# Moving one wait and one table load at the ends of a transformer kernel's feed-forward phases

## What is computed

```python
def swiglu(h, w_in, w_out):
    gate, up = jnp.split(h @ w_in, 2, axis=-1)
    return (jax.nn.silu(gate) * up) @ w_out

for l in range(DEPTH):
    h = h + 0.5 * swiglu(rms_norm_2(h, ffn1_norm[l]), ffn1_w_in[l], ffn1_w_out[l])
    h = h + hybrid_mixer(rms_norm_2(h, mix_norm[l]), ...)
    h = h + 0.5 * swiglu(rms_norm_2(h, ffn2_norm[l]), ffn2_w_in[l], ffn2_w_out[l])
return rms_norm_2(h, final_norm)[:, META:]
```

## Time and profile before

| | |
|---|---|
| median of 3 runs | 2420.91 us (2420.75 to 2426.59) |
| profiled execution | 2424.67 us, its span 2422.7 us |
| TensorE busy, share of the span | 93% |
| TensorE's weight loads | 86% |
| VectorE, ScalarE | 68%, 49% |
| mean granted clock of TensorE | 0.961 of full speed |
| the four feed-forward phases' first products start at | 984.27, 1505.44, 1714.84, 2216.71 us |
| TensorE idle before them | 2.64, 4.06, 4.06, 4.05 us |
| TensorE idle at the two mixers' starts | 5.58 us each |
| other idle times of TensorE within the two mixers | 17, together 17.8 us |

### The profile page before, as it was taken

The page is one execution under the profiler, slowest core; times in us unless marked ns, Lnnn a source line. Parts: engine busy times, 40 slices in busy tenths (PEclk is TensorE's granted clock), DMA queues, the critical chain, the costliest instruction groups (busy, mean ns, idle before and its releaser), DMA issues. The chain is left out here.

```text
span 2422.7 us, 40671 instructions
## 1 busy us (share of the span) xinstructions
PE 2242.9 (93%) x16709; PEld 2090.7 (86%) x16709; DVE 1639.5 (68%) x2201; ACT 1186.6 (49%) x1656; POOL 100.4 (4%) x133
## 2 busy tenths in 40 slices
PE   6978899969888998899999998999999999998998
PEld 6868778859677886899888898999999888898998
DVE  5674588843847885777665656777777665656786
ACT  4744466733646774533356445333433346545333
POOL 2022000000000000000300000000000210000000
PEclk8989899989999999999999999999999999999999
DMA  8420379939125994545542234545454553344552
GB/s 219 138 87 20 108 265 338 345 102 209 36 71 203 342 335 148 175 157 174 159 142 88 89 130 163 176 162 186 138 193 156 149 154 103 105 157 160 188 189 72
DMA packets 257020, 395.53 MB, mean 163 GB/s; under 512 B 16937, under 2 KB 204194, under 8 KB 256866
## 3 DMA queue, kind: packets, MB, share of 16 engines
q1 hardware_dynamic: 251616, 380.09, 46.7%
q0 software_dynamic: 4880, 13.13, 3.1%
q10 hardware_dynamic: 370, 0.11, 0.0%
HBM read 385.43 MB, written 7.86 MB: 162 GB/s over the span
## 5 line engine op out<-in xcount | busy, mean ns | idle before, releaser
L315 PE MATMUL psum_banks<-source_high,weights_high 128*128 128x272 f32 (+1 forms) x2656 | 785.5, 296 | 56.5 <-DVE weights_low L1813 23.5
L317 PE MATMUL psum_banks<-source_high,weights_low 128*128 128x272 f32 (+1 forms) x2656 | 770.7, 290 | 0.0
L316 PE MATMUL psum_banks<-source_low,weights_high 128*128 128x272 f32 (+1 forms) x2656 | 770.6, 290 | 0.0
L315 PEld LDWEIGHTS psum_banks<-source_high,weights_high 128*128 128x128 f32 x2656 | 513.5, 193 | 66.1 <-DVE weights_low L1813 26.1
L316 PEld LDWEIGHTS psum_banks<-source_low,weights_high 128*128 128x128 f32 x2656 | 514.0, 194 | 0.8
L317 PEld LDWEIGHTS psum_banks<-source_high,weights_low 128*128 128x128 f32 x2656 | 513.3, 193 | 0.0
L1813 DVE TENSOR_TENSOR weights_low<-weight_ring,weights_high 128x2048 fp32r<-128x2048 f32 x104 | 239.3, 2303 | 186.1 <-ACT weights_high L1806 185.6
L694 DVE TENSOR_TENSOR weights_low<-weight_ring,weights_high 128x2048 fp32r<-128x2048 f32 x131 | 292.8, 2287 | 73.7 <-ACT weights_high L688 73.5
L688 ACT ACTIVATE weights_high<-weight_ring 128x2048 fp32r<-128x2048 f32 x131 | 242.4, 1912 | 191.9 <-PE psum_banks L317 181.8
L1806 ACT ACTIVATE weights_high<-weight_ring 128x2048 fp32r<-128x2048 f32 x104 | 198.5, 1909 | 43.8 <-PE psum_banks L317 34.6
L315 PE MATMUL psum_banks<-hidden_high,weights_high 128*128 128x272 f32 (+1 forms) x736 | 213.0, 289 | 0.0
(11 more groups left out here) (494 smaller groups left out, 3794.0 us busy)
## 6 DMA issues: line engine op xcount, KB each, us to landing
weight_ring<-ffn_w_in SPq DMA_DIRECT2D x88, 1024.0 KB, 6.6
weight_ring<-w_in SPq DMA_DIRECT2D x48, 1024.0 KB, 5.3
weight_ring<-ffn_w_out SPq DMA_DIRECT2D x44, 1024.0 KB, 4.9
weight_ring<-moe_w_down SPq DMA_DIRECT2D x24, 1024.0 KB, 6.9
weight_ring<-moe_w_gate SPq DMA_DIRECT2D x44, 512.0 KB, 4.8
weight_ring<-moe_w_up SPq DMA_DIRECT2D x44, 512.0 KB, 6.5
weight_ring<-gdn_w_in SPq DMA_DIRECT2D x16, 1024.0 KB, 5.8
more_ring<-moe_w_gate SPq DMA_DIRECT2D x32, 512.0 KB, 5.0
```

Source lines behind the costliest of these rows:

```text
L315: pe.matmul(out, w_hi, x_hi, start=start, stop=False)
L316: pe.matmul(out, w_hi, x_lo, start=False, stop=False)
L317: return pe.matmul(out, w_lo, x_hi, start=False, stop=stop)
```

## The change

It has two parts, both in `ffn_phase`.

TensorE's wait for the root (`relay.std`) stood ahead of the first chunk's gate products. It now stands between the two halves of the up products, ahead of the only ones that write bank 3.

ScalarE takes a root of one number per partition into a new buffer `junk` that nobody reads. It stands after the last chunk's silu and before the wait for the first finished block of `h`. The load of the root's table is put in front of it.

```diff
         squares = pr.sb(ctx, "squares", [P, KT, L])
+        junk = pr.sb(ctx, "junk", [P, 1])
...
         def gate_up_first(pe):
-            pe.wait_ge(relay.std.sem, relay.std.at(1))
             pe.wait_ge(lo_n.sem, lo_n.at(place(0, "gate") + 1))
             products(pe, 0, "gate", 0)
             products(pe, 0, "gate", 1)
             pe.wait_ge(lo_n.sem, lo_n.at(place(0, "up") + 1))
-            for m in range(2):
-                products(pe, 0, "up", m).then_inc(hm.sem, 1)
+            products(pe, 0, "up", 0).then_inc(hm.sem, 1)
+            pe.wait_ge(relay.std.sem, relay.std.at(1))
+            products(pe, 0, "up", 1).then_inc(hm.sem, 1)
...
                 for c in range(2 * pairs + 1, n_chunks):
                     step(c, c)
+                act.activation(junk[:, :], pr.eps[EPS], ACT.Sqrt)
                 for k in range(KT):
                     act.wait_ge(ad.sem, ad.at(8 * last + k + 1))
```

## The result

The changed kernel takes 2398.72 us (median of 4 runs, 2395.76 to 2399.76) against 2421.03 before (4 runs). The ratio is 0.9899, with a 95% interval of 0.9886 to 0.9913, so it is 1.0% faster: 22.3 us by the medians, 24.5 (21 to 28) by the ratio. Every ratio is to runs of the kernel before that were taken beside the runs in question. The forecast was 2397.5 in a range of 2392.5 to 2409. A second set of runs beside later experiments gave 2398.1 us and 0.9905 (0.9889 to 0.9922).

What follows compares the result with a forecast made beforehand. TensorE's own work plus its idle places were taken to bound the kernel. Wait 12.8, clock 6.7 and table loads 3.9 sum to 23.4 us: 2401.3 for the profiled execution, 2397.5 against the median, range 2392.5 to 2409.

Steps and rivals of the forecast that it cites:

- The wait: Four feed-forward starts: TensorE's 14.8 us wait for the root shrinks to 0.5 us each, gaining 12.8 us.
- the lower bound: Feed-forward starts: TensorE restarts at the earliest 0.30 us after its last sum, as ScalarE does.
- The clock: Behind the three longer gaps at feed-forward starts: the fall to half clock goes, gaining 6.7 us.
- The table loads: Loads moved ahead of the roots at two mixers' starts and the end: 1.29 us each, together 3.9 us.
- That rival (2393.6): Three table loads that count: each moved load frees as much again, 3.9 us more, because ScalarE empties first; chance 0.03.
- the one of a preload without effect: Dummy root: a load is put before each root anyway, so 19.5 us gained, 2401.4; chance 0.07.
- VectorE as the next limit: Feed-forward starts: VectorE's 5.22 us idle time is used up, leaving 0.9 us margin at TensorE's second chunk.
- rival 2: VectorE takes the wait's place: TensorE waits for weights_low or scaled halves within 15 us of phase start; 2417.0, chance 0.06.
- The panel: Feed-forward starts: a panel issued at the block's start lands in 5.1 us, so panels don't hold VectorE up.
- The slower rival: Mixers' short idle times meet the clock at worse moments, 1.5 us per new fall; about 2434 with 20, chance 0.02.

Runs made afterwards that it cites:

- the gap was filled: Kernel before, wait in its old place, TensorE making 15 or 27 unread products into an unused bank while it waits: 2414.49 us, ratio 0.9973.
- the second reciprocal: Unread second reciprocal on VectorE behind the first in each feed-forward phase: changed kernel 2406.72 us, ratio 0.9933; kernel before 2422.68 us, ratio 1.0001.
- the root first: Changed kernel with root and reciprocal ahead of the up panel's split in feed-forward phases, plus a dummy root in the mixers: 2403.54 us, ratio 0.9912.
- TensorE's later start: Changed kernel with TensorE waiting for the up panel's high part before the gate products, a gap of 2.26 us: 2403.88 us, ratio 0.9939.
- the kernel with the filled mixers: Changed kernel with five unread products in the 2.68 us in which TensorE waits at tile 10 of each mixer: 2399.38 us, ratio 0.9902.

## Why the prediction was right, point by point

- **The wait.** 12.8 us were forecast from a restart 0.5 us behind the last sum. It is 0.32 us in all four places, so that the term is 13.5 (2.32 + 3.74 + 3.74 + 3.73). I had called it the least supported number; the lower bound, ScalarE's 0.30 us in the same block, was nearly the value.
- **The clock.** 6.7 us forecast, about 6.8 in the two traces (1.6 + 2.7 + 2.5), and 6.5 (4.4 to 8.7) by itself where the gap was filled. But one of my grounds was weak. I took the first phase, at full clock behind 2.64 us, as a sign that such a gap is safe. It was not: the same 2.64 us brought a fall at the same place with the preload alone, and 2.26 us brought one in four. What holds is that 0.32 us brought none, in the four phases here and in those of seven more traces in which TensorE goes on that soon.
- **The table loads.** 3.9 us forecast; the three waits shrank by 1.28 us each, 3.8. Alone the preload gave 5.3 us in its waits, since the third phase counts then, 5.6 by the medians and 7.3 by the ratio (4.8 to 9.7). The drain that the Trainium skill ("ScalarE: Activation LUTs", "What ACT_TABLE_LOAD costs") adds to a load is not in the trace: the wait at a mixer's start went from 5.58 to 4.29 us, one load's length. That rival (2393.6) is refuted, and so is the one of a preload without effect: only two of the six loads are left in front of a root.
- **VectorE as the next limit.** The scaled half was forecast for +11.4 us from the block's start. It came at +11.2 (1710.52 + 0.43, block start 1699.72), and TensorE did not wait for it: its second chunk starts at 1711.9, 0.95 us later. The margin of 0.9 was right there, and the second reciprocal confirms it. I missed the last phase. It has 256 tokens instead of 272, which makes TensorE's chunk 6% shorter, but a panel's split on VectorE takes 2.29 us all the same. There the margin is 0.4 us, and a new wait of 0.6 us stands 26 us behind the phase's start, at the first down products. It goes when VectorE is given more room, by the root first or by TensorE's later start. So rival 2 was true in a mild form, at another place than its sign named, and by a fortieth of the gain.
- **The panel.** "One issued at the block's start lands in 5.1 us" was read from the third phase before, and does not hold for the first phase after. ScalarE stood idle there until the panel had landed, 6.4 us behind its issue:

```profile
986.02 1.93 ACT L689 ACTIVATE weights_high<-weight_ring 128x2048 fp32r<-128x2048 f32 x1 [2.33 <-DMA weight_ring<-ffn_w_in]
```

```profile
weight_ring<-ffn_w_in SPq DMA_DIRECT2D x1, 1024.0 KB, 6.4
```

It cost nothing, since 0.8 us of margin were left. But in the first phase the panel took 6.1 to 7.1 us in all nine traces in which TensorE works from the block's start, and 5.0 to 5.1 in the four in which it stands idle first. In the kernel with the filled mixers that left a margin of 0.2 us. So in the first phase a TensorE at work goes with a later panel, which the prediction put at nothing; what makes the panel late is not shown.
- **The slower rival.** Nothing of it showed in the time. But the mixers' falls did stand at other places from kernel to kernel, as it supposed. Whether they make up the spread of 3 to 11 us between executions of one kernel is not shown: of 19 executions of the kernel before, the slowest (2427.19 us) and the fastest (2418.83) have the same mean granted clock, 0.963.
- **The sum.** 23.4 us forecast for the profiled execution, 23.7 found, 22.3 between medians and 24.5 by the ratio. The terms' errors (+0.7, +0.1, -0.1, and -0.6 for the wait that I missed) are each smaller than the spread. That the first and the last nearly cancel is luck.

## What to carry to other kernels

A wait that protects one buffer belongs in front of the first instruction that writes that buffer. Read from the bank numbers, and not from the names of the stages, who needs the result; then follow which engine's idle time pays for the head start, since its end is the next limit. Where TensorE stands idle for some us, price the half clock behind it as well, as a chance and not as a certainty for the shorter gaps: here it made more than a quarter of the gain. And look again at when the transfers land, since the panel issued at the start of the first phase came more than 1 us later when TensorE worked at once. A dummy activation that loads a table early is free only where ScalarE's idle time covers load and dummy, 1.5 us; check what is queued behind it there, because one step in front of a needed split it costs its full length.

## What the runs showed of the hardware that I had not expected

- The clock behind idle times of like length was not the same: half behind one of four gaps of 2.64 us (first phase with the preload alone) and full behind three (first phase before, without and with the second reciprocal, and third phase with the preload alone); half behind one of four gaps of 2.26 us, 18 of 22 of 2.68 us in the mixers, and all eight of 4.06 us (4.05 in the last phase).
- TensorE's first product starts 0.32 us behind the end of its last product of the block before. ScalarE starts at the same time, 0.30 us behind it.
- A root of one column takes 0.20 us on ScalarE.
- A panel of 1 MB that is issued alone at a phase's start landed after 4.9 to 5.2 us in the second and third phases of every trace, but after 6.1 to 7.1 in the first phase wherever TensorE worked from its start, and after 6.3 and 6.7 in the last phase of the two kernels with filled mixers.
